# Neighbourhood attention: scores as three fp32r passes, and another share of the copies of turned probabilities

## What is computed

```python
q = p[..., :d].reshape(b, rows, GRID_W, nh, hd) * scale
...
s_loc = jnp.einsum('bqhd,bikhd->bhqik', q_r, k_band).astype(jnp.float32) + bias
s_ctx = jnp.einsum('bqhd,blhd->bhql', q_r, k_c).astype(jnp.float32)
s = jnp.concatenate([s_loc.reshape(b, nh, GRID_W, band), s_ctx], axis=-1)
prob = jax.nn.softmax(s, axis=-1).astype(v.dtype)
```

## Time and profile before

| | |
|---|---|
| median of 3 runs | 2634.4 us (2632.09 to 2634.77) |
| the profiled execution | 2633.1 us |
| its span, first to last instruction | 2631.3 us |
| busy: PE, PEld | 2580.2 us, 2114.9 us |
| busy: DVE, ACT, POOL | 2008.5 us, 602.3 us, 112.3 us |
| neighbourhood loop, from scores of pair 2 to the output product | 957.15 to 1042.41 us |

### The profile page before, as it was taken

How to read it: one execution, slowest core, us unless ns; L and a number is a source line. 1 busy time by engine, 2 the same in 40 slices (tenths; PEclk the granted TensorE clock), 3 DMA queues, 4 the chain that set the end, 5 groups by cost and what they waited for, 6 DMA issues and landing times.

```text
span 2631.3 us, 31820 instructions
## 1 busy us (share of the span) xinstructions
PE 2580.2 (98%) x13052; PEld 2114.9 (80%) x13052; DVE 2008.5 (76%) x2304; ACT 602.3 (23%) x1284; POOL 112.3 (4%) x93
## 2 busy tenths in 40 slices
PE   6999999999999999999999999999999999999999
PEld 4788888888877876898788888788888888878887
DVE  4688786977657747978876888787687778978776
ACT  2112121311221147221110332421021023252101
POOL 0000000000000011100000001010000000200000
PEclk8999999999999999999999999999999999999999
DMA  7543242444543633555555545355465555434653
GB/s 272 176 136 105 97 143 75 135 154 160 176 160 113 204 76 90 177 183 190 169 182 185 183 146 175 112 193 184 160 212 188 180 174 170 161 127 160 200 183 122
DMA packets 252001, 420.35 MB, mean 160 GB/s; under 512 B 35520, under 2 KB 93312, under 8 KB 251856
## 3 DMA queue, kind: packets, MB, share of 16 engines
q1 hardware_dynamic: 248352, 410.09, 47.8%
q0 software_dynamic: 2272, 5.07, 0.6%
q10 hardware_dynamic: 1232, 3.15, 0.3%
HBM read 417.22 MB, written 1.05 MB: 159 GB/s over the span
## 4 chain that ended last, share of the span: by engine, by line
PE 91%; DVE 4%; ACT 2%; DMA 1%; issue 1%; POOL 0%; ACTq 0%; DVEq 0%
PE psum L500 87%; PE psum L514 3%; PE psum L809 1%; DVE wgt_lo L1745 1%; DMA raw<-ada_w 1%; DVE wgt_hi L1743 1%; ACT W L1199 1%; ACT L1199 0%; DVE W L2220 0%; ACT n_prob_b L1199 0%; ACT xh L1199 0%; DVE xl L1766 0%; DMA cst<-consts 0%; PE psum L658 0%; DVE xl L1754 0%
## 5 line engine op out<-in xcount | busy, mean ns | idle before, releaser
L1745 DVE TENSOR_TENSOR wgt_lo<-raw,wgt_hi 128x2048 fp32r<-128x2048 f32 (+2 forms) x336 | 761.9, 2268 | 11.5
L500 PE MATMUL psum<-wgt_hi,xh 128*128 128x512 f32 (+1 forms) x1744 | 683.1, 392 | 2.9 <-DVE xl L1754 1.4
L500 PE MATMUL psum<-wgt_hi,xl 128*128 128x512 f32 (+1 forms) x1744 | 676.5, 388 | 0.0
L500 PE MATMUL psum<-wgt_lo,xh 128*128 128x512 f32 x1728 | 669.7, 388 | 0.0
L1743 DVE CAST wgt_hi<-raw 128x2048 fp32r<-128x2048 f32 (+2 forms) x336 | 411.6, 1225 | 122.3 <-PE psum L500 116.0
L500 PEld LDWEIGHTS psum<-wgt_hi,xh 128*128 128x128 f32 x1744 | 327.9, 188 | 73.3 <-issue 7.8
L500 PEld LDWEIGHTS psum<-wgt_hi,xl 128*128 128x128 f32 x1744 | 327.7, 188 | 66.3
L500 PEld LDWEIGHTS psum<-wgt_lo,xh 128*128 128x128 f32 x1728 | 325.1, 188 | 62.7
L500 PE MATMUL psum<-wgt_hi,yh 128*128 128x512 f32 x928 | 364.8, 393 | 1.5 <-DVE wgt_lo L1745 1.0
L500 PE MATMUL psum<-wgt_hi,yl 128*128 128x512 f32 x928 | 361.6, 390 | 0.0
L500 PE MATMUL psum<-wgt_lo,yh 128*128 128x512 f32 x928 | 361.4, 389 | 0.0
(11 more groups left out here) (236 smaller groups left out, 2178.0 us busy)
## 6 DMA issues: line engine op xcount, KB each, us to landing
raw<-mlp_w SPq DMA_DIRECT2D x64, 1024.0 KB, 5.3
raw<-w_in SPq DMA_DIRECT2D x60, 1024.0 KB, 5.0
raw<-ada_w SPq DMA_DIRECT2D x48, 1024.0 KB, 5.3
raw<-ffn_w_gate SPq DMA_DIRECT2D x40, 1024.0 KB, 5.1
raw<-ffn_w_up SPq DMA_DIRECT2D x40, 1024.0 KB, 5.1
raw<-ffn_w_down SPq DMA_DIRECT2D x40, 1024.0 KB, 5.0
raw<-ret_w_in SPq DMA_DIRECT2D x24, 1024.0 KB, 5.1
raw<-nat_w_in SPq DMA_DIRECT2D x12, 1024.0 KB, 5.2
```

The source lines that it names most:

```text
L500: return pe.matmul(o, l, r, start=start_, stop=stop, skip_group_check=True)
L1745: v.tensor_tensor(wgt_lo[:, s % RING, :size], r, wgt_hi[:, s % RING, :size], ALU.subtract).then_inc(split_done.sem, split_done.up())
```

## The change

Scores: `nk` and `nq` are now each held as a rounded high and a low part. For each pair and part (high x high, high x low of the keys, low of the queries x high) and each of the two heads there is one fp32r matmul of 512 columns, where there was one fp32 matmul for a head; the heads alternate inside a part. For this
- ACT's eviction of a key unit writes `nk_hi` in fp32r, and DVE subtracts (`low(("nk", t), ...)`, eight instructions of 128 x 512, placed after `scale_row` and ahead of `keep_up(("nq", 7))`). The key units now belong to DVE ("dve").
- queries are still written in fp32 by ACT; then for each block b ACT rounds them (`nat_queries(b)`, 128 x 256) and DVE subtracts (128 x 256). Block 0 is done ahead of the first scores, block 1 after the values, block b + 1 at n mod 4 = 1 on ACT and n mod 4 = 2 on DVE.
- `nat_scores` waits for `queries_split` at the first pair of a block.

Copies: `turned_by_dve` is now true for j = 1 of n mod 4 = 0, 1 and 3, three of eight tiles; it was true for j = 1 of odd n, two of eight.

No transfer is added or moved.

```diff
-            return n % 2 == 1 and j == 1
+            return n % 4 != 2 and j == 1
...
-            features_by_tokens("nk", D, KT, 2 * T, "act", wb, after=lambda b: ask_modulation(1, 5, b), ready=ready)
+            features_by_tokens("nk", D, KT, 2 * T, "dve", wb, after=lambda b: ask_modulation(1, 5, b), ready=ready)
...
                 if n % 4 == 0:
-                    pe.wait_ge(out_of(("nq", b)), emptied(("nq", b)))
-                for j in range(2):
-                    r = 2 * NAT_HD * half + NAT_HD * j
-                    ins = mm(psum[:, 2 * (n % 2) + j, :], nq[r:r + NAT_HD, b, qt * P:(qt + 1) * P], nk[r:r + NAT_HD, b, :], True, True)
+                    pe.wait_ge(out_of(("nk", b)), emptied(("nk", b)))
+                    pe.wait_ge(queries_split.sem, queries_split.at(b + 1))
+                q = slice(qt * P, (qt + 1) * P)
+                for part in range(3):
+                    for j in range(2):
+                        r = slice(2 * NAT_HD * half + NAT_HD * j, 2 * NAT_HD * half + NAT_HD * (j + 1))
+                        ins = mm(psum[:, 2 * (n % 2) + j, :], nq_lo[r, b, q] if part == 2 else nq_hi[b][r, q],
+                                 nk_lo[b][r, :] if part == 1 else nk_hi[r, b, :], part == 0, part == 2)
...
-                act_(nk[:, t, :], bank_of(("nk", t))).then_inc(act_out.sem, act_out.up())
+                act_(nk_hi[:, t, :], bank_of(("nk", t))).then_inc(act_part.sem, act_part.up())
...
+            def nat_queries(b):
+
+                act.wait_ge(out_of(("nq", b)), emptied(("nq", b)))
+                act_(nq_hi[b], nq[:, b, :]).then_inc(queries_high.sem, queries_high.up())
...
+            nat_queries(0)
             nat_exp(0)
             nat_exp(1)
...
+            nat_queries(1)
             for n in range(2, N_PAIRS + 2):
                 nat_turned(n - 2)
                 if n < N_PAIRS:
                     nat_exp(n)
+                if n % 4 == 1 and n // 4 + 1 < KT:
+                    nat_queries(n // 4 + 1)
...
             dve.wait_ge(x_scaled.sem, x_scaled.now())
+            for t in range(KT):
+                low(("nk", t), nk_lo[t], nk_hi[:, t, :])
+
+            def nat_queries(b):
+
+                dve.wait_ge(queries_high.sem, queries_high.at(b + 1))
+                v.tensor_tensor(nq_lo[:, b, :], nq[:, b, :], nq_hi[b], ALU.subtract).then_inc(queries_split.sem, queries_split.up())
...
             keep_up(("nq", KT - 1))
+            nat_queries(0)
             nat_rowmin(0)
             nat_rowmin(1)
...
                 if 0 <= n - 2 < N_PAIRS and turned_by_dve(n - 2, 1):
                     nat_turned(n - 2)
+                if n % 4 == 2 and n // 4 + 1 < KT:
+                    nat_queries(n // 4 + 1)
```

More of the change, by code:

```diff
@@ L202, in build @@
         scores_full = signal("scores_full")
+        queries_high = signal("queries_high")
+        queries_split = signal("queries_split")
         rowmin_ready = signal("rowmin_ready")
@@ L374, in build @@
         n_inv, n_out = W[:, 12288:12544], X[:, 3, D - T:D]
+        nk_hi = W_fp32r[:, 2048:6144].rearrange("p (a b) -> p a b", a=KT)
+        nk_lo = [(yl if b % 2 else yh)[:, b // 2 * 2 * T:(b // 2 + 1) * 2 * T] for b in range(KT)]
+        nq_lo = W_fp32r[:, 0:2048].rearrange("p (a b) -> p a b", a=KT)
+        nq_hi = [W_fp32r[:, 12288:12544]] + [W_fp32r[:, 10240 + T * (b % 2):10240 + T * (b % 2 + 1)] for b in range(1, KT)]
         n_zero = [W[:, 12544:12800], X[:, 3, 512:512 + T], x_rest[:, 6, 0:T], x_rest[:, 6, 0:T]]
```

## The result

| | before | after |
|---|---|---|
| median of 14 runs each, side by side | 2633.59 us (2631.6 to 2635.21) | 2640.42 us (2636.35 to 2644.62) |
| ratio | | 1.0027, 95% interval 1.0020 to 1.0034 |
| profiled execution / its span | 2633.1 / 2631.3 us | 2638.86 / 2637.1 us |
| from scores of pair 2 to the output product | 85.26 us | 1047.89 - 958.07 = 89.82 us |

The change makes the kernel slower by 0.27%, and the interval leaves no doubt of the direction. The forecast was 2633.5 us and "the same", with "slower" at 0.20. The median lies 3.9 us above the forecast's own range (2630.5 to 2636.5) and inside the wide one (2628.5 to 2641.5) only because that one holds the rival of 2641, which is not what happened: the way there is none of the four rivals.

The account below looks back on a forecast made before the run. TensorE was taken to bound the kernel, with DVE's order limiting the gain. Loop -3.0, keys +1.2 and queries +0.85 gave -0.95 us, so 2633.5 us against a median of 2634.4; own range 2630.5 to 2636.5.

Parts of the forecast that it names:

- the wide one: Whole kernel: the range 2628.5 to 2641.5 us, given a chance of 0.80.
- part 2: Neighbourhood loop, DVE's order walked with a third copy and the query subtraction: stretches 8.74, 9.91, then 10.40; 3.0 us saved.
- Part 1, the slot: Scores of a pair on TensorE: three fp32r passes, heads side by side, take 0.86 us instead of 1.06.
- heads one after another: Rival for the scores: fp32r passes of two heads don't overlap, slot 1.57, +17.8 us, 2652 us; chance 0.12.
- not fp32r: Rival for the scores: passes on 32 rows run at two clocks a column, slot 1.49, 2648 us; chance 0.03.
- loads not hidden: Rival for the scores: two of three weight loads exposed, slot 1.22, +6.5 us, 2641 us; chance 0.05.
- 0.5 was the sign to look for: Second transposes of every C step, from n = 12: TensorE waits about 0.5 us for DVE's copy.
- Part 3, splitting the keys: Key stage: the first two DVE subtractions delay the third weight block's split, +1.2 us, bounds 0 and 1.4.
- Part 4, splitting the queries: Before the first scores: rounding and subtraction of block 0 become a new link, +0.75, with the first pairs +0.85 us.
- the 0.1 of the first two pairs: First scores, two pairs on four groups of rows: about 0.1 us more than the 1.25 before.
- The sum: Whole kernel: -3.0 + 1.2 + 0.85 = -0.95 us against the profiled execution; forecast 2633.5 us.
- TensorE stays the bound: Rival for the loop: DVE's lateness is absorbed, every stretch takes 9.91, -3.5 us, 2631 us; chance 0.13.

Follow-up runs that it names:

- the scores alone: Against the changed kernel: old share of the copies, two of eight by DVE, with the three fp32r passes kept; 2633.3 us, ratio 1.0008.
- the keys ahead: Against the changed kernel: one keep_up ahead of the key subtractions, so DVE splits the third key block first; 2639.1 us, ratio 1.0021.

## Why the prediction was wrong

Step by step, in the order of the prediction.

The step that failed is in part 2: the price of DVE's new subtraction, 0.42 us, taken without what POOL does at that moment. It measured 1.08 and 2.72 us where it met POOL. With it failed an assumption that stands in no part, that a wait of TensorE costs its own length.

**Part 1, the slot.** Forecast 0.86, measured 0.89. TensorE in after, one pair:

```profile
988.02 0.50 PE L506 MATMUL psum<-W_fp32r 32*128 32x512 f32 x2
...
988.35 0.40 PE L506 MATMUL psum<-yl,W_fp32r 32*128 32x512 f32 x2
...
988.58 0.40 PE L506 MATMUL psum<-W_fp32r 32*128 32x512 f32 x2
```

The next work starts at 988.91: 0.33 + 0.23 + 0.33. Each row is a pair of heads (x2), so the two run side by side in fp32r too, and the rivals "heads one after another" (1.57) and "not fp32r" (1.49) are out. So is "loads not hidden" (1.22): with 0.23 to 0.33 from one part to the next there is no room for a pass of 0.213 and an exposed load of 0.18. The rule of the Trainium skill (TensorE: Matmul & The Clock Gate, Part 3, The mechanism), by which a load overlaps only when the row group differs, would give that 1.22; the rows differ from it. The 0.03 were missed in the price of a pass, taken as 0.213 where 0.23 is seen; it makes up 0.12 of the 0.15 by which the second stretch, 10.06, is over 9.91.

**Part 2, the walk.** Right in its times where nothing was held: 8.74 against 8.78, 10.40 against 10.43, no gain at the end (11.59 from the scores of pair 30 to the output product before, 1047.89 - 1036.29 = 11.60 now). In part that is luck: TensorE's own stretch is 10.06 to 10.11 and not 9.91, and DVE's lateness adds 0.32 to 0.37 and not 0.49, with the idle time for the copy at 0.16 in the profile where 0.5 was the sign to look for; DVE's busy time is 9.03, not 9.4. The step that failed is one number in it: "one subtraction of 128x256 (0.42 to 0.43, about 0.35 to the next independent start)". The rows it was taken from are those of a subtraction whose source is in PSUM; the new one has both in SBUF, and next to POOL's 3.46 it costs up to 3.69. Of its seven places in the loop two met a window of POOL in the trace of after and three in that of the scores alone; when POOL starts depends on when the transfer of the bias lands. The prediction took DVE's durations as DVE's own, and POOL as an engine that "prepares the bias". The price of the failed step: 2.3 and 0.67 us of DVE's time in after, in a stretch where the walk itself said that DVE is late.

**Its consequence, which no part had.** A wait of TensorE was priced at its length. Here waits of 2.4 us lengthened two stretches by 6.55, of which about 4.3 us, by the estimate above, came on top at half clock. The rivals dealt with the slot or with DVE's lateness, never with what TensorE does after a long wait.

**Part 3, splitting the keys.** Right in mechanism, near in size. TensorE took the third block 865.31 - 853.22 = 12.09 after the second, before 11.07 (854.04 to 865.11): +1.0, forecast +1.2. The prediction read the start of the third block as 865.0, so it counted a slack of 0.1 where there was 0.2; the wait is 0.90. The wait of after and what stood ahead of the split:

```profile
860.51 0.68 DVE L1773 TENSOR_TENSOR yh<-psum,W_fp32r 128x512 fp32r<-128x512 f32 x1
861.11 0.68 DVE L1773 TENSOR_TENSOR yl<-psum,W_fp32r 128x512 fp32r<-128x512 f32 x1
861.71 1.22 DVE L1762 CAST wgt_hi<-raw 128x2048 fp32r<-128x2048 f32 x1
...
865.31 0.50 PE L506 MATMUL psum<-xh,wgt_hi 128*128 128x512 f32 x1 [0.90 <-DVE wgt_lo L1764]
```

**Part 4, splitting the queries.** Right for the link: scores start 1.29 after the start of the last eviction instead of 0.48, +0.81 for +0.75.

```profile
911.61 0.38 ACT L1209 ACTIVATE W<-psum 128x256 f32<-128x256 f32 x1 [2.49 <-PE psum L506]
911.89 0.41 ACT L1209 ACTIVATE W_fp32r<-W 128x256 fp32r<-128x256 f32 x1
912.33 0.43 DVE L2097 TENSOR_TENSOR W_fp32r<-W,W_fp32r 128x256 fp32r<-128x256 f32 x1 [2.85 <-ACT W_fp32r L1209]
912.90 0.62 PE L506 MATMUL psum<-W_fp32r 32*128 32x512 f32 x4 [1.33 <-DVE W_fp32r L2097]
```

Wrong in sign for the 0.1 of the first two pairs: four heads on four groups of rows (x4) need hardly more than two. From their start to TensorE's next work it is 1.02 (912.90 to 913.92) where it was 1.19 (911.76 to 912.95): 0.17 less instead of 0.1 more. "The later seven splits are a step or more ahead of need and are in part 2" is true of when they are asked for and false of when they end: at 1004.20 TensorE waited for one.

**The sum.** Of the profiled executions: -0.8 ahead of the second key block (853.22 and not 854.04; the same 0.8 is there at 473 us already, ahead of all that the change touches), +1.0 to the third, +0.1 from there to the last query eviction, +0.8, -0.2 up to pair 2, +4.6 in the loop and +0.3 behind it make +5.8. The loop's +4.6 is -2.7 and +7.2. **TensorE stays the bound**, the rival at 0.13, is what comes about once the subtraction leaves DVE (10.11 and 10.06). What was set too low is the chance of an unnamed cost: 0.20 for "slower" held only rivals about the slot.

## What to carry to other kernels

Price a new instruction by where its operands lie, not only by its shape, and look at which other engine is at work at that moment: a DVE instruction with both sources in SBUF, put into a loop in which POOL works in long pieces, must be priced by POOL's piece. Small elementwise work between SBUF buffers can go to the engine that would hold it up, in its queue behind the long pieces, at its slower 0.73 instead of 0.41. And a standstill of TensorE is not always paid at its length: here the clock fell behind those of 1.9 us and more in the loop, for 10 us and more, and behind 1.74 to 1.96 outside it in some executions and not in others. Ask for each queue that gets nearer to its limit what the longest single wait is, not only the mean. Last, look in the trace before for instructions that take longer than their like (1.22 and 3.53 us here): they show a clash before it is built in.

## What the runs showed of the hardware

- DVE's subtraction of 128x256, SBUF to SBUF, alone 0.41 us: begun while POOL subtracts 128x1536 (3.46 us), it ended 0.27 to 0.29 us after POOL did, in seven such meetings (1.08 and 2.72 us long in after; 1.86, 3.69 and 1.08 with the scores alone; 1.05 and 2.80 with the keys ahead). DVE instructions with an operand in PSUM kept their 0.69 and 0.73 beside the same POOL work. A cast of 128x2048, SBUF to SBUF, 1.22 us alone, took 3.53 and 4.53 beside it in before.
- TensorE's granted clock went to half (1.2 GHz) 0.6 to 1.4 us after it had resumed from standstills of 1.93, 1.94, 2.90 and 3.03 us in the loop, and was back 10.24 us later; with the keys ahead it fell during a standstill of 1.94 and was back 13.7 us later. In the loop it stayed at 2.4 GHz after 1.52 and 1.65. Outside the loop it fell behind 3.40 in 13 of 13 traces, 1.96 in 6 of 12, 1.89 or 1.90 in 5 of 13 and in 4 of 12, and 1.74 in 1 of 13, for 3.4 us or more.
- Two fp32r passes of 512 columns on two different 32 rows of the array take 0.23 us together, the weight loads hidden, and three such pairs with entering and leaving the split array 0.89 us; where it was one fp32 matmul each, 1.06.
- POOL's subtraction of 128x256 takes 0.73 us.
